# Attention of the decode samples and the output merge woven into one stage of 16 steps

## What is computed

```python
def _sb_block(q, k, v, q_pos, k_pos, bias):
    z = jnp.einsum('bqhd,bkhd->bhqk', q, k) * (SB_HEAD_DIM ** -0.5) + bias[None, :, None, None]
    vis = k_pos[None, :] < q_pos[:, None]
    log_keep = jnp.where(vis, jax.nn.log_sigmoid(-z), 0.0)
    after = lax.cumsum(log_keep, axis=3, reverse=True) - log_keep
    a = jnp.where(vis, jnp.exp(jax.nn.log_sigmoid(z) + after), 0.0)
    return jnp.einsum('bhqk,bkhd->bqhd', a, v)
```

```python
def _merge(h, o_gdn, z_gdn, o_sb, z_sb, gdn_norm_g, w_out, ln_g, ln_b):
    og = _rmsnorm(o_gdn, gdn_norm_g).reshape(B, L, GDN_VW) * jax.nn.silu(z_gdn)
    osb = o_sb.reshape(B, L, SB_W) * jax.nn.silu(z_sb)
    mix = jnp.einsum('ble,ed->bld', jnp.concatenate([og, osb], axis=-1), w_out)
    return _layernorm(ALPHA * h + mix, ln_g, ln_b)
```

## Time and profile before

| | |
|---|---|
| median of 3 runs | 2574.44 us (2569.6 to 2577.78) |
| the profiled execution | 2578.45 us, its span 2576.5 us |
| PE busy over the span | 2332.3 us (91%) |
| DVE, ACT, POOL busy | 1190.5, 887.4, 748.1 us |
| bytes moved by DMA | 225.58 MB, mean 88 GB/s |
| granted clock of PE, mean | 0.956 |

### The profile page before, as it was taken

The page is one execution under the profiler, slowest core; times in us unless marked ns, Lnnn a source line. Parts: engine busy times, 40 slices in busy tenths (PEclk is TensorE's granted clock), DMA queues, the critical chain, the costliest instruction groups (busy, mean ns, idle before and its releaser), DMA issues. The chain is left out here.

```text
span 2576.5 us, 42715 instructions
## 1 busy us (share of the span) xinstructions
PE 2332.3 (91%) x16321; PEld 1458.8 (57%) x16321; DVE 1190.5 (46%) x1972; ACT 887.4 (34%) x2032; POOL 748.1 (29%) x703
## 2 busy tenths in 40 slices
PE   6999999999999999699999668989898968869997
PEld 4666444444444444588888555556565645544443
DVE  2323155755600000455555136878787844433342
ACT  3232132232200000233333027878787832221110
POOL 3444010010000000344443035656555510003544
PEclk9999999999999999899999559999999989999999
DMA  6333213312223430511111110000000059993441
GB/s 175 102 108 106 51 34 49 70 34 51 69 56 46 85 88 35 193 51 51 52 51 43 47 41 1 34 18 23 29 1 18 2 183 332 338 349 127 139 158 63
DMA packets 159247, 225.58 MB, mean 88 GB/s; under 512 B 16320, under 2 KB 95377, under 8 KB 154488
## 3 DMA queue, kind: packets, MB, share of 16 engines
q1 hardware_dynamic: 159096, 223.50, 29.6%
HBM read 154.55 MB, written 68.91 MB: 87 GB/s over the span
## 5 line engine op out<-in xcount | busy, mean ns | idle before, releaser
L506 PE MATMUL ps<-hT,wc 128*128 128x512 f32 (+1 forms) x1920 | 708.1, 531 | 9.5 <-PEq L124 5.9
L506 PEld LDWEIGHTS ps<-hT,wc 128*128 128x128 f32 x1920 | 336.9, 191 | 380.4 <-issue 378.1
L1571 POOL TENSOR_TENSOR f_a<-f_a,f_keep 128x384 f32<-128x384 f32 (+4 forms) x352 | 310.5, 897 | 236.6 <-DVE f_keep L1539 229.3
L1539 DVE TENSOR_TENSOR_SCAN f_keep<-f_keep,ps 128x384 f32<-128x384 f32 (+4 forms) x352 | 340.2, 1011 | 3.8 <-ACT f_keep L1494 3.7
L332 PE MATMUL ps<-wt,hT_now 128*128 128x344 f32 x816 | 242.1, 457 | 4.3 <-DMA wt<-w_in 4.3
L2033 PE MATMUL ps<-m_w,m_mT 128*128 128x512 f32 x544 | 237.8, 596 | 0.0
L1441 PE MATMUL ps<-con,f_a 128*128 128x128 f32 x1216 | 176.5, 287 | 55.3 <-POOL f_a L1571 32.8
L1494 ACT ACTIVATE f_keep<-ps,small 128x384 f32<-128x384 f32 (+4 forms) x352 | 193.7, 612 | 69.0 <-PE ps L1424 40.9
L1441 PEld LDWEIGHTS ps<-con,f_a 128*128 128x128 f32 x1216 | 135.6, 145 | 134.2 <-POOL f_a L1571 69.3
L332 PEld LDWEIGHTS ps<-wt,hT_now 128*128 128x128 f32 x816 | 155.4, 192 | 83.5 <-DMA wt<-w_in 4.9
L1502 ACT ACTIVATE f_a<-ps,small 128x384 f32<-128x384 f32 (+4 forms) x352 | 194.6, 623 | 0.0
(11 more groups left out here) (277 smaller groups left out, 3040.7 us busy)
## 6 DMA issues: line engine op xcount, KB each, us to landing
j_kp<-cache_k SPq DMA_DIRECT2D x128, 256.0 KB, 4.2
j_v<-cache_v SPq DMA_DIRECT2D x128, 256.0 KB, 4.7
chan<-y SPq DMA_DIRECT2D x12, 1088.0 KB, 6.4
chan<-pre SPq DMA_DIRECT2D x12, 1088.0 KB
wc<-w_in SPq DMA_DIRECT2D x24, 512.0 KB, 8.4
d_ld<-chan SPq DMA_DIRECT2D x16, 768.0 KB, 5.6
h_rows<-hg SPq DMA_DIRECT2D x17, 512.0 KB, 5.0
m_hh<-h_rows SPq DMA_DIRECT2D x17, 512.0 KB, 3.3
```

What stands on the lines that cost most here:

```text
L506: m = pe.matmul(ps[:, ci, 0:n], wc[k][:, c, :], hT[:, c, c0:c0 + n], start=(c == 0), stop=(c == KC - 1))
L1539: dve.tensor_tensor_scan(w, w, ps[:, NIL_BANK, 0:1].broadcast_to([P, c1 - c0]), before, ALU.mult, ALU.bypass).then_inc(scanned, 1)
L1571: pool.tensor_tensor(w, w, keep[(2 * s + e) % KEEPS][:, off + c0 + 1:off + c1 + 1], ALU.mult).then_inc(weighed, 1)
```

## The change

The two stages become one, `samples_and_merge`, of 16 steps without loops of the sequencers. In step `j` the samples' step `j` runs, and the merge's tile `j - 1` is multiplied; the sample tile comes last. On PE each group of 4 key transposes is followed by one product of the merge, now over 2 PSUM banks for the keys (ACT copies out the even groups, DVE the odd ones); 4 products stand between the transposes of the weights and the scores, and 4 after the values. The output has one pair of banks instead of two. The scores are laid out in four strips of 32 rows, one for each head pair `c`, with 16 rows per sample in a strip; the two samples add up in it. `qb`, the bias rows, the mask constant and the columns of `values` follow that layout. SP reads the page number again for the value pages, with bounds. The sample outputs go from SBUF straight to the gating and are no longer stored and loaded again. `rows28`, `sc` and `tails` are allocated only for the first two stages. The diff, cut to its core:

```diff
-    parts.append((c // STEPS == i // NS) & (c >= 0) & (c % STEPS < i % STEPS))
+    parts.append((c // STEPS == i // 16 % 2) & (c >= 0) & (c % STEPS < i % STEPS))
...
-        self.rows28 = self.sb("rows28", [28, CB, P])
-        self.sc = self.sb("sc", [P, CB, 28])
-        self.tails = self.sb("tails", [P, CB, 27])
...
+            h = 2 * (i // 4) + i % 2
...
+def samples_and_merge(p, own):
...
+    J = G * ITS
+    LAST = J
+    K_BANK, Z_BANK, A_BANK, M_BANK, O_BANK, Y_BANK = 0, 2, 3, 4, 5, 6
...
+            def load_keys(j, s):
+                if s == 0 and j == 0:
+                    sp.wait_ge(table, START + 16)
+                after(sp, k_turned, 8 * (j - 1) + 4 * s + 4)
+                for i in range(GP):
+                    at_page = 2 * PAGES * (j // G) + PAGES * s + GP * (G - 1 - j % G) + i
+                    page = sp.value_load(pages[0:1, at_page:at_page + 1], min_val=0, max_val=p.n_phys - 1)
+                    sp.dma_start(kp[s][:, i:i + 1, :], io["cache_k"][0, ds(page, 1)].rearrange("a t h d -> t a (h d)")).then_inc(k_loaded[s], 16)
+
+            def load_values(j):
+                after(sp, av_done, j - 1)
...
+            def load_tile(i):
+                b = i % 2
+                after(sp, s_["sb_gated"], i - 1)
...
+            def load_h(i):
+                after(sp, s_["summed"], 2 * (i - 1))
+                sp.dma_start(hh[i % 2][:, :], p.h_rows[i + 1 if i < LAST else 0]).then_inc(h_loaded[i % 2], 16)
...
+            load_keys(0, 0)
+            load_keys(0, 1)
+            load_tile(0)
+            sp.dma_start(gn[:, :], row(io["gdn_norm_g"][0])).then_inc(g_loaded, 16)
+            for c in range(0, KC, KC // 2):
+                sp.dma_start(w[:, c:c + KC // 2, :], wo[:, c:c + KC // 2, :]).then_inc(w_loaded, 16)
+            load_keys(1, 0)
+            load_keys(1, 1)
+            load_values(0)
+            load_tile(1)
+            load_h(0)
+            sp.dma_start(lng[:, :], row(io["ln_out_g"][0])).then_inc(rows_loaded, 16)
+            sp.dma_start(lnb[:, :], row(io["ln_out_b"][0])).then_inc(rows_loaded, 16)
+            for j in range(J):
+                if j and j + 1 < J:
+                    load_keys(j + 1, 0)
+                if j:
+                    load_h(j)
+                if j + 2 <= LAST:
+                    load_tile(j + 2)
+                if j and j + 1 < J:
+                    load_keys(j + 1, 1)
+                if j >= 2:
+                    store(j - 2)
+                if j + 1 < J:
+                    load_values(j + 1)
+            load_h(LAST)
...
+            def turn_keys(j, s, c):
+                n = 8 * j + 4 * s + c
+                if c == 0:
+                    pe.wait_ge(k_loaded[s], START + 64 * j + 64)
+                after(pe, kT_out[c % 2], n // 2)
+                for i in range(GP):
+                    m = pe.transpose(ps[:, K_BANK + c % 2, i * PAGE:(i + 1) * PAGE], kp[s][:, i, c * P:(c + 1) * P], p.ident)
+                m.then_inc(k_turned, 1)
...
+            def scores(j):
+                after(pe, gated, j)
+                if j % G == 0:
+                    pe.wait_ge(new_gated, START + j // G + 1)
+                for e in range(2):
+                    pe.wait_ge(kT_out[e], START + 4 * j + 4)
+                for s in range(2):
+                    for c in range(PAIRS):
+                        m = pe.matmul(ps[32 * c:32 * c + 32, Z_BANK, :], qb[s][:, 32 * c:32 * c + 32], kT[s][:, c, :], start=(s == 0), stop=(s == 1))
+                m.then_inc(z_acc, 1)
...
+            def turn_mix(i):
+                pe.wait_ge(s_["mixed"], START + i + 1)
+                after(pe, s_["mT_ready"], i)
+                if i and (i - 1) % G == 0:
+                    pe.wait_ge(at_out, START + i)
+                for c in range(GH):
+                    m = pe.transpose(ps[:, M_BANK, c * P:(c + 1) * P], mix[i % 2][:, c * P:(c + 1) * P], p.ident)
+                m.then_inc(s_["turned"], 1)
+
+            def product(i, f, c):
+                if f == 0 and c == 0:
+                    pe.wait_ge(s_["mT_ready"], START + i + 1)
+                    pe.wait_ge(s_["sb_gated"], START + i + 1)
+                    pe.wait_ge(w_loaded, START + 32)
+                if c == 0:
+                    after(pe, s_["summed"], 2 * i + f - 1)
+                m = pe.matmul(ps[:, Y_BANK + f, :], mT[i % 2][:, c, :], w[:, c, 512 * f:512 * f + 512], start=(c == 0), stop=(c == KC - 1))
+                if c == KC - 1:
+                    m.then_inc(s_["y_acc"], 1)
+
+            for j in range(J):
+                for s in range(2):
+                    for c in range(PAIRS):
+                        turn_keys(j, s, c)
+                        if j:
+                            product(j - 1, 0, 4 * s + c)
+                if j:
+                    turn_weights(j - 1)
+                if j % G == 0:
+                    new_scores(j // G)
+                if j:
+                    for c in range(4):
+                        product(j - 1, 1, c)
+                scores(j)
+                if j:
+                    values(j - 1)
+                turn_mix(j)
+                if j:
+                    for c in range(4, KC):
+                        product(j - 1, 1, c)
+            turn_weights(J - 1)
+            for c in range(KC):
+                product(LAST - 1, 0, c)
+            values(J - 1)
+            for c in range(4):
+                product(LAST - 1, 1, c)
+                m = pe.transpose(ps[:, K_BANK + b // 4, (b % 4) * P:(b % 4 + 1) * P], ob[:, b // 2, (b % 2) * P:(b % 2 + 1) * P], p.ident)
+            turn_mix(LAST)
+            for c in range(4, KC):
+                product(LAST - 1, 1, c)
+            for f in range(2):
+                for c in range(KC):
+                    product(LAST, f, c)
...
+            for j in range(J):
+                keys_out(j, 0)
+                if j == 0:
+                    squares(0)
+                keys_out(j, 1)
+                if j % G == 0:
+                    act.wait_ge(new_acc, START + j // G + 1)
+                act.wait_ge(z_acc, START + j + 1)
+                gates(ps[:, Z_BANK, :], keep[j % 2][:, :], a[j % 2][:, :]).then_inc(gated, 1)
+                mix_out(j)
+                squares(j + 1)
+            mix_out(LAST)
...
+            for j in range(J):
+                if j >= 2:
+                    add_h(j - 2, 1)
+                    statistics(j - 2)
+                if j % G == 0:
+                    queries(j // G)
+                if j == 0:
+                    keys_out(j, 0)
+                    mean_squares(j)
+                else:
+                    mean_squares(j)
+                    keys_out(j, 0)
+                if j >= 2:
+                    normalize(j - 2)
+                if j == 0:
+                    keys_out(j, 1)
+                mixes(j)
+                if j:
+                    keys_out(j, 1)
+                gate_channels(j)
+                if j:
+                    weights_out(j - 1)
+                if j % G == 0:
+                    new_keys(j // G)
+                if j:
+                    add_h(j - 1, 0)
+                weigh(j)
+                if j and j % G == 0:
+                    outputs(j // G - 1)
+            add_h(LAST - 2, 1)
+            statistics(LAST - 2)
+            weights_out(J - 1)
+            mean_squares(LAST)
+            normalize(LAST - 2)
+            mixes(LAST)
+            add_h(LAST - 1, 0)
...
+            for i in range(LAST + 1):
+                gate(i)
+                if i == 2:
+                    pool.wait_ge(rows_loaded, START + 32)
+                if i >= 2:
+                    finish(i - 2)
+            finish(LAST - 1)
+            finish(LAST)
...
-            out = MergeInputs(p, st)
-            p.run(sample_attention, samples, out)
-            p.run(merge, out)
+            p.run(samples_and_merge, samples)
```

More of the change, by code:

```diff
@@ L1639, in after, with tile_loads @@
         def after(eng, sem, n):
-            if not isinstance(n, int) or n > 0:
+            if n > 0:
                 eng.wait_ge(sem, START + n)
+        def tile_loads(i):
+            return 64 * (i // 2) + (64 if i < LAST else 48)
         @block.sync
         def _(sp):
[L1646 to L1661, removed]
+            def load_keys(j, s):
[8 more added lines that the diff above has]
+                after(sp, av_done, j - 1)
@@ L1676, in _ @@
+            load_h(LAST)
+            for i in range(LAST - 2, LAST + 1):
+                store(i)
+            sp.wait_ge(stored[0], START + 16 * (NT // 2 + 1))
+            sp.wait_ge(stored[1], START + 16 * (NT // 2))
         @block.tensor
         def _(pe):
[L1678 to L1688, removed]
@@ L1745, in values @@
                 m.then_inc(av_done, 1)
-            def step(it, g):
-                j = G * it + g
-                turn_keys(it, g, 0)
-                turn_keys(it, g, 1)
-                if not (isinstance(j, int) and j == 0):
```

(54 more changed lines are left out.)

440 lines of the change are left out of this document (143 added, 297 removed).

## The result

The changed kernel is slower by 0.9%: 2597.35 us (median of 4 runs, 2593.66 to 2598.79) against 2572.77 (4 runs, 2569.6 to 2577.78), ratio 1.0092, 95% interval 1.0071 to 1.0112. The forecast was 2512, the range ended at 2542, and the sign is wrong. The profiled execution took 2593.66 us with a span of 2591.5 us, so the trace is 77.5 us longer than the 2514 of my sum.

A forecast was written before the change was run, and what follows sets the result against it. Samples bound by DMA, merge by PE; woven, PE sets 22.8 us a step. Opening to 2121, body 342 + 6, tail 31.8, end 13.0 give 2514, saving 62.5 from the median 2574.4: 2512, range 2500 to 2542.

The forecast's parts named there:

- my sum: Whole kernel: opening to 2121, body to 2469, tail to 2501, end at 2514 us.
- Order on DVE is the tight place: DVE's key copies in each step: groups 3 and 7 just get their banks, at 3.9 and 9.1 us.
- Two banks pace the keys: Rival, DVE's key copies: late by 1 to 2 us a step, 15 to 30 us back, 2527 to 2542; chance 0.17.
- each us of it is 15 us: The 16-step stage: a wait recurring once a step costs 15 us for each us of it.
- The slower rival: SP's queue sets the pace: slower from 1.5 us a page; at 1.8, 2644 us; chance 0.04.
- Opening: Loads before step 1: 8.4 MB from 2093.6 end at about 2119; step 1 starts in effect at 2121.
- plain steps: Steps without new tokens: transposes, weights, scores, values and a merge tile sum to 22.1 us of PE.
- the backlog: Loads still queued after the opening, 21 MB until step 2's second-sample keys: some 3 us more in step 2.
- Scores in strips: Scores on PE in four strips: 16 instructions take 1.85 us a step, bounds 1.72 and 1.97, instead of 3.58.
- the rival had 28: Rival, scores on PE: the strips don't run four abreast, 28 us more, 2540; chance 0.05.
- Interleaving at nothing: Key transposes between merge products on PE: no added cost; bound 0.8 us a step for weight loads not hidden.
- The DMA rival: DMA binds the steps: rate falls to 250 GB/s, 25.2 us a step, 36 us more, 2548; chance 0.06.

The follow-up runs named there:

- e1: The changed kernel with POOL's gain and bias on 8 of the 1024 columns, the rest left out: 2517.08 us, ratio 0.9773 to the kernel before.
- e2: The changed kernel with DVE's `mix` of tile j moved ahead of `normalize` of tile j - 2, all work kept: 2522.14 us, ratio 0.9791 to the kernel before.
- e7: The kernel with `mix` ahead of `normalize`, scores again in two halves of 64 columns with the old layout: 2550.72 us, ratio 0.9915 to the kernel before.
- e6: The changed kernel with `mix` and gating ahead of `normalize` and tile 1 loaded ahead of `w_out`: 2520.34 us, ratio 0.9793 to the kernel before.

## Why the prediction was wrong, point by point

- **The step that failed: "Order on DVE is the tight place".** I had the right place and even the right group ("group 7 wants the bank at 9.1 us. Again just met"), but took `mixes` at some 1.2 us, the duration of a stage in which POOL stands at that moment. Behind `normalize` it takes 5.38. DVE and POOL were compared with the step by their sums, 11.6 and 7.5 us; which of their instructions would run side by side was never asked, though my own order has POOL's gain released by the end of `normalize` and `mixes` starting there. The Trainium skill's rule (SBUF — State Buffer, as above) speaks against this change, and the prediction doesn't weigh it.
- **The rival "Two banks pace the keys"** named the symptom (PE idle before key transposes, released by DVE's copy) and priced it at 1 to 2 us a step. It was 3.2 to 3.6. Two banks alone don't cost it: e1 and e2 have two banks and wait 1.6 us in all. Whether more banks would have hidden the slow `mix` wasn't tried; all eight are in use.
- **The clock** was left out of the price of such a wait. The slower work at the half clock is 24.5 of e2's 71.3 us: "each us of it is 15 us" was too little, 46.1 us of waits made 71.3.
- **The slower rival** was given to SP's queue. In the trace of after eight value pages go out in 7.95 to 8.71 us, 1.0 to 1.1 each, well below the 1.5 from which it would decide. The right sign came from another mechanism, which had no chance in my list.
- **Opening.** Step 1 began at 2120.2 for my 2119, and that is luck in part. The first key page went out at 2090.3, 3.3 us before the 2093.6 of the count, because the stages before ended earlier in this execution (over all runs here it goes out between 2088.3 and 2095.3); from there it took 29.9 us instead of 25.4, at 306 GB/s, so 9.1 MB for my 8.4. What I missed besides is ACT's queue; I looked at the DMA engines, SP and DVE. `squares(1)` waits for a tile that comes late in SP's order, with the key copies behind it.
- **What held, seen in e2,** which is the change with one call moved. Span 2520.2 for the 2514 of the sum. Step 1 starts at 2121.7 (2121 in effect), 0.7 late, with the same luck (first key page at 2091.4). It takes 37.1 us for 22.8, 14.3 more. Steps 2 to 15 take 316.6 for 14 x 22.8 + 6 = 325.2, 8.6 less: plain steps 21.9 (22.1 forecast); two of each four take 23.5 to 23.7, together 3.5 more than plain ones, where I had 2.9 and 0.8 for `queries` on one of four; and the backlog of 3 us in step 2 isn't there; I take it that the long step 1 has covered it. 0.7 + 14.3 - 8.6 = 6.4.
- **Scores in strips:** 2314.03 to 2315.78, 1.75 us for 16, between my bounds of 1.72 and 1.97; e7 gives 28.6 us for the whole, for which the rival had 28. The Trainium skill (TensorE: Matmul & The Clock Gate, Measured speedup vs the span model) has 3.07 times for four row strips; carried over to these four column strips that would give 2.24. The trace doesn't agree for this shape: 16 x 0.43 / 1.75 is 3.9 abreast.
- **Interleaving at nothing:** right. In the chain of e2 four transposes and two products repeat as 0.44 + 0.86 with nothing between. Its body is 99.5% busy. The DMA rival is out too: share 0.86 and 267 GB/s in that window, and no wait for pages in it, only in the opening.

So of the 77.5 us between 2514 and 2591.5, 71.3 are `mix` behind `normalize` with the clock that it costs, and 6.2 the opening, less what the steps were better.

Open: why the clock is at 0.50 after twelve of these stops and at 1.00 after two of 3.20 us, when others of 3.19 to 3.22 are among the twelve; no run varied it alone. Loading all of `w_out` ahead wasn't tried.

## What to carry to other kernels

When two stages are laid over each other, a table of sums by engine isn't enough for DVE and POOL: list for every DVE instruction with two operands in SBUF what POOL does at that time, and take POOL's whole instruction as its price if it reads SBUF. The mend is an order, not less work: put those instructions where POOL waits, and leave copies out of PSUM for the time when it is busy. And a wait once a step in front of PE is priced with the clock that follows, here 1.5 times the idle time.

## What the runs showed of the hardware

- A DVE instruction with two operands in SBUF that starts while a POOL instruction with both operands there runs ends shortly after it: products of 0.34 us took 2.44 and 2.49 and ended 0.15 us after POOL's, a gating of 0.68 took 2.51 and ended 0.55 after. POOL's stayed at 2.34 to 2.39. A DVE copy from PSUM kept its 0.69, and an add with one operand in SBUF and one in PSUM its 0.67 to 0.69 (e6).
- Four column strips of 32 with 512 columns run 3.9 abreast; two halves of 64 ran 1.9 abreast.
- Of 14 stops of 3.19 to 3.60 us in front of PE, twelve were followed by a granted clock of 0.50, two of 3.20 us by 1.00.
- SP issues eight value pages, whose numbers it reads with bounds, in 7.95 to 8.71 us, 1.0 to 1.1 each; the eight key pages of the earlier trace rows, read without bounds, took 6.81, 0.85 each.
